# Two transformer blocks in sequence on one core: where an attention phase begins and ends among the projections around it

## The reference

```
mod = silu(c) @ ada_w + ada_b                    # shift, scale, gate
h = rmsnorm(x) * (1 + scale) + shift             # latent and context tokens
px, pc = split(h @ w_in)                         # q, k, v of A, B, C, and a gate
ya = softmax(rope(rmsnorm(q)) @ rope(rmsnorm(k)).T) @ v       # A: all keys
yb = softmax(q @ gathered_k.T + bias, q @ kc.T) @ v           # B: 2-D neighbourhood
yc = softmax(rope(q) @ banded_k.T, q @ kc.T, sink) @ v        # C: sliding window
x = x + gate * ((concat(ya, yb, yc) * silu(px[9])) @ w_out)   # context alike in layer 0
```

## Time and profile before

| | |
|---|---|
| profiled execution | 2545.05 us, of which the span of the trace 2543.2 |
| PE busy | 2439.3 us, 96% of the span |
| DVE, ACT, POOL busy | 1352.0, 950.8, 541.5 us |
| share of PE in the chain that ended last | 81% (DVE 8%, ACT 4%, issue 3%, POOL 2%) |
| projection of block 1 (L2380) on PE | 555.6 us |
| attention on PE (L575, L603) | 159.1 and 150.7 us |
| mean granted clock of TensorE | 0.992 of full speed |

### The profile page before, as it was taken

How to read it: one execution, slowest core, us unless ns; L and a number is a source line. 1 busy time by engine, 2 the same in 40 slices (tenths; PEclk the granted TensorE clock), 3 DMA queues, 4 the chain that set the end, 5 groups by cost and what they waited for, 6 DMA issues and landing times.

```text
span 2543.2 us, 38062 instructions
## 1 busy us (share of the span) xinstructions
PE 2439.3 (96%) x14758; PEld 1982.2 (78%) x14758; DVE 1352.0 (53%) x2731; ACT 950.8 (37%) x1751; POOL 541.5 (21%) x530
## 2 busy tenths in 40 slices
PE   6999999999998999999999999999999999999998
PEld 4777877878887778778778668888888767888887
DVE  3667756765407663666827745333335953533333
ACT  4464254452324542645335334222225333422222
POOL 2212222122243122221365232000003331100001
PEclk9999999999999999999999999999999999999999
DMA  7402422224124034132524112323323212223322
GB/s 270 145 2 75 174 63 72 84 94 178 57 79 166 26 125 158 39 133 95 190 85 145 51 57 68 106 77 114 98 81 103 71 53 72 83 84 107 100 83 75
DMA packets 66900, 250.36 MB, mean 98 GB/s; under 512 B 7969, under 2 KB 11553, under 8 KB 57377
## 3 DMA queue, kind: packets, MB, share of 16 engines
q1 hardware_dynamic: 62960, 236.36, 27.4%
q0 software_dynamic: 3248, 11.54, 1.4%
q10 hardware_dynamic: 512, 0.03, 0.0%
HBM read 243.67 MB, written 4.19 MB: 97 GB/s over the span
## 4 chain that ended last, share of the span: by engine, by line
PE 81%; DVE 8%; ACT 4%; issue 3%; POOL 2%; DVEq 1%; ACTq 0%; DMA 0%; SPq 0%; POOLq 0%
PE ps L2560 34%; PE ps L2380 20%; PE ps L575 5%; PE ps L603 5%; PE ps L643 4%; PE ps L2537 4%; DVE ps L1960 2%; ACT probs L797 2%; PE ps L2264 1%; PE ps L2361 1%; POOL split_panels_first L1059 1%; PE ps L2509 1%; PE ps L2399 1%; PE ps L2577 1%; PE ps L2309 0%
## 5 line engine op out<-in xcount | busy, mean ns | idle before, releaser
L2560 PE MATMUL ps<-h_split,split_panels 128*128 128x512 f32 x2928 | 685.7, 393 | 1.8 <-ACT projected L1506 0.8
L2560 PEld LDWEIGHTS ps<-h_split,split_panels 128*128 128x128 f32 x2928 | 545.9, 188 | 126.9 <-issue 13.7
L2380 PE MATMUL ps<-h_split_first,split_panels_first 128*128 128x512 f32 x2808 | 555.6, 355 | 9.0 <-DVE h_split_first L1828 4.9
L2380 PEld LDWEIGHTS ps<-h_split_first,split_panels_first 128*128 128x128 f32 x2808 | 453.5, 191 | 85.4 <-issue 7.8
L1059 POOL TENSOR_TENSOR split_panels_first<-panels_first,split_panels_first 128x1024 fp32r<-128x1024 f32 (+1 forms) x104 | 233.3, 2244 | 581.2 <-ACT split_panels_first L1249 581.2
L1905 DVE TENSOR_TENSOR split_panels<-panels,split_panels 128x1024 fp32r<-128x1024 f32 (+2 forms) x171 | 192.6, 1126 | 297.9 <-ACT split_panels L1257 294.2
L1257 ACT ACTIVATE split_panels<-panels 128x1024 fp32r<-128x1024 f32 (+2 forms) x210 | 204.3, 974 | 344.9 <-PE ps L2560 343.6
L1740 DVE SCALAR_TENSOR_TENSOR ps<-modulation_panels,silu_c,ps 128x256 f32<-128x256 f32 x480 | 225.1, 487 | 30.5 <-issue 2.1
L2560 PE MATMUL ps<-ffn_hidden_split,split_panels 128*128 128x512 f32 x990 | 225.0, 389 | 0.0
L2560 PEld LDWEIGHTS ps<-ffn_hidden_split,split_panels 128*128 128x128 f32 x990 | 185.8, 188 | 38.6
L1070 POOL TENSOR_TENSOR probs_turned<-probs_turned,probs 128x512 f32<-128x512 f32 x30 | 41.8, 1392 | 769.8 <-ACT probs L1449 769.8
(11 more groups left out here) (300 smaller groups left out, 2931.5 us busy)
## 6 DMA issues: line engine op xcount, KB each, us to landing
modulation_panels<-in_ada SPq DMA_DIRECT2D x64, 1024.0 KB, 5.0
panels<-in_w SPq DMA_DIRECT2D x88, 512.0 KB, 3.5
panels_first<-in_in SPq DMA_DIRECT2D x72, 512.0 KB, 5.8
panels<-in_in SPq DMA_DIRECT2D x42, 512.0 KB, 3.6
panels_first<-in_out SPq DMA_DIRECT2D x32, 384.0 KB, 3.0
panels<-in_w SPq DMA_DIRECT2D x32, 384.0 KB, 3.1
panels<-in_w SPq DMA_DIRECT2D x32, 320.0 KB, 2.8
panels<-in_out SPq DMA_DIRECT2D x16, 512.0 KB, 3.4
```

The source lines that it names most:

```text
L2380: ins = mm(at0, split1[:, s, w, c, :], hs1[:, h, c, lo:e], start=c == 0 and i == 0, stop=c == KC - 1 and i == 2)
L2560: ins = mm(out, split[:, n % SPLIT, a, c - base, :], moving(b, c), start=first and i == 0 and j == 0, stop=last and i == len(chunks) - 1 a ...
```

## The change

Four edits, all in the first block.

1. ACT: in the last block of a projection phase of A, B or C, the last `take_mod` and the two exponentials of unit 0 now stand ahead of the eviction of that block; behind it only the panel is rounded.
2. PE: the last modulation sum stands ahead of the scores of unit 0 and no longer behind the block's last chunk. `make_plan` numbers the turned tiles in the new order.
3. PE, order in the first steps: in A and C the turning of unit 0 stands ahead of the scores of unit 1 (`i == 1`); in all three mixers the outputs of unit 0 stand ahead of the turning of unit 1 (`i == 2`). In B the wait for the eviction moves from the scores of unit 1 to those of unit 2.
4. PE, exit: the latent products of two chunks of the next projection (three matmuls of 512 columns each, `latents_ahead`) go one ahead of the turning of the last unit, one between the last two outputs. The context products of these chunks stay where they were.

```diff
@@ make_plan
-        if before:
-            behind(before)
         if values_second and i == 1:
             step["values"] = values(groups[0][0], None)
+        (behind(before) now stands ahead of it)
@@ attention_pe
+                i = u["i"] if u else None
+                if m != "B" and i == 1:
+                    turn_probs_pe(pe, prev, o)
+                if i == 1:
+                    pe.wait_ge(mod_taken, ada_no[spare[l, last - 1]] + 1)
+                if i == (2 if m == "B" else 1):
+                    pe.wait_ge(proj_taken, NSEQ[l, last] + 1)
                 if u:
                     scores_pe(pe, u, o)
                 if u and step["values_first"]:
                     turn_values_pe(pe, step, o)
-                if prev:
+                if i == 2:
+                    turn_weights_pe(pe, old)
+                    outputs_pe(pe, old, o)
+                if u is None and old:
+                    latents_ahead(pe, l, NEXT[m], 0 if prev else 1)
+                if prev and not (m != "B" and i == 1):
                     turn_probs_pe(pe, prev, o)
...
-                if old:
+                if old and i != 2:
                     turn_weights_pe(pe, old)
                     outputs_pe(pe, old, o)
+        def latents_ahead(pe, l, m, c):
+            b = PHASES[m][0]
+            k, n = NSEQ[l, b], main_no[IN1, l, b]
+            if c == 0:
+                pe.wait_ge(rest1_done, n + 1)
+                pe.wait_ge(proj_taken, k - 1)
+            for i, (w, h) in enumerate(((0, 0), (0, 1), (1, 0))):
+                nc.tensor.matmul(bank(k % 2), split1[:, n % SPLIT1, w, c, :], hs1[:, h, c, 0:SEQ], start=c == 0 and i == 0, stop=False)
@@ attention_act
-                if u:
+                if u and (u["i"] > 0 or not u["in_sets"]):
                     exponentials_act(act, u, o)
@@ projected (ACT)
                         load_table(ACT.Exp)
+                        take_mod(spare[l, b - 1])
+                        first = next(step["unit"] for step in plans[l, m][0] if step["unit"])
+                        exponentials_act(act, first, Off(None))
                     act.wait_ge(proj_ready, k + 1)
@@ project (PE)
-                        block_chunk(l, b, n, c)
+                        block_chunk(l, b, n, c, m != "A" and j < 0 and c < AHEAD)
-                    if (l, b - 1) in spare:
+                    if (l, b - 1) in spare and not (m in "ABC" and b == PHASES[m][1] - 1):
                         sum_mod(spare[l, b - 1])
-                if m == "B":
-                    pe.wait_ge(proj_taken, k + 1)
-                    pe.wait_ge(mod_taken, ada_no[spare[l, b - 1]] + 1)
             def first_scores(l, m, k):
-                pe.wait_ge(*parts_made(ada_no[spare[l, PHASES[m][1] - 2]]))
+                sum_mod(spare[l, PHASES[m][1] - 2])
```

More of the change, by code:

```diff
@@ L166, in make_plan @@
         step = dict(unit=u, prev=before, old=two_back, values=[], values_first=values_second)
+        if before:
+            behind(before)
         if values_second and i == 1:
             step["values"] = values(groups[0][0], None)
-        if before:
-            behind(before)
         if values_second:
@@ L662, in attention_pe @@
                 u, prev, old = step["unit"], step["prev"], step["old"]
-                if m == "B" and u and u["i"] == 2:
+                i = u["i"] if u else None
[5 more added lines that the diff above has]
+                    pe.wait_ge(proj_taken, NSEQ[l, last] + 1)
+                if m == "B" and i == 2:
                     pe.wait_ge(values_taken, steps[0]["values"][1]["w"] + 1)
-                if m != "B" and u and u["i"] == 1:
-                    pe.wait_ge(proj_taken, NSEQ[l, last] + 1)
-                    pe.wait_ge(mod_taken, ada_no[spare[l, last - 1]] + 1)
                 if u:
@@ L831, in two_dit_blocks @@
         ADA1, ADA2, IN1, OUT1 = "ada1", "ada2", "in1", "out1"
+        NEXT = {"A": "B", "B": "C", "C": "G"}
+        AHEAD = 2
         second = [(ADA2, l, i) for l in range(DEPTH) for i in range(N_ADA2)]
@@ L1317, in projected @@
                             round_gated(l, c)
-                    if (l, b - 1) in spare and b != 1:
+                    if (l, b - 1) in spare and b != 1 and not (m in "ABC" and b == PHASES[m][1] - 1):
                         take_mod(spare[l, b - 1])
@@ L2371, in _, with block_chunk @@
             turn_mod(0)
-            def block_chunk(l, b, n, c):
+            def block_chunk(l, b, n, c, ahead=False):
                 k, s = NSEQ[l, b], main_no[IN1, l, b] % SPLIT1
@@ L2378, in block_chunk @@
                     for at0, lo, e in ((bank(k % 2), 0, SEQ), (bank(2 + k % 2, 0, CTX), SEQ, TOK)):
-                        if lo < n:
+                        if lo < n and not (ahead and lo == 0):
                             ins = mm(at0, split1[:, s, w, c, :], hs1[:, h, c, lo:e], start=c == 0 and i == 0, stop=c == KC - 1 and i == 2)
```

## The result

| | before | after |
|---|---|---|
| median of 9 runs each | 2549.18 us (2544.89 to 2556.15) | 2561.58 us (2556.82 to 2564.64) |
| ratio of the runs | | 1.0041, interval [1.0032, 1.0049] |
| profiled execution, span | 2545.05, 2543.2 us | 2561.93, 2560.1 us |
| mean granted clock | 0.992 | 0.987 |

The changed kernel is slower, by 0.3 to 0.5%. The forecast was 2558.8 us in a range of 2547 to 2569, with 0.76 for a difference within 0.5%. The time came out as forecast; one term of the sum, the clock, did not.

What follows compares the result with a forecast made beforehand. PE was taken as the bound, busy 2439.3 of 2543.2 us. Entries +10.7, exits -8.2 and clock +6.0 sum to +8.5 us, on the median of 2550.32 giving 2558.8, range 2547 to 2569.

Steps and rivals of the forecast that it cites:

- A, forecast +3.84 each: Entries of A0 and A1: PE waits for ACT's exponentials and DVE's copies, losing 3.84 us at each.
- B, +0.55 and -0.84: Entries of B0 and B1: PE waits 2.5 us for POOL's weights; +0.55 us at B0, -0.84 at B1.
- C, +1.86 and +1.43: Entries of C0 and C1: new PE waits for exponentials, weights and a DVE copy; +1.86 and +1.43 us.
- Exits, -8.2: Six phase exits: moved chunks of 0.73 us each fill PE's two gaps per exit; -8.2 us in all.
- A reading beside it: Context matmuls in a row at the exits: 11 to the microsecond, 0.09 us each, so they lose nothing.
- The clock, 4 falls x 1.5 = +6.0: Half-clock stretches behind the new long entry gaps: four at 1.5 us, +6.0 us, with 0 and 9 as ends.
- (b): Every new gap of 2.4 us and more brings a 1.7 us clock fall, six: +12.7, 2563.0 and up; chance 0.14.
- two of the four: Of the four gaps of 2.4 to 2.5 us (A0, A1, B0, B1), two bring a clock fall of 1.5 us.
- (a): The clock stays up behind the new gaps: 2545.05 + 2.5 us, or 2552.8 by the median; chance 0.22.
- (c): Exits give nothing, as PE then waits for DVE's modulation products in the next projection: 2567.0 us; chance 0.06.
- (d): Entries gain too, if DVE copies unit 0 before unit 1's row extremes: entries -13, exits -8, 2529 us; chance 0.04.

Runs made afterwards that it cites:

- copy-first variant: Changed kernel with DVE's copy of the turned group and weights of unit 0 ahead of unit 1's row extremes in A and C: 2546.68 us, ratio 0.9993 to before.
- exits-only trace: Kernel before plus only the two latent chunks of the next projection placed among the last unit's steps: 2538.73 us, ratio 0.9965 to before.
- entries-only kernel: Changed kernel without the chunks moved ahead at the exits: 2563.14 us, ratio 1.0063 to the kernel before.

## Why the prediction was right, and where it was off

- **A, forecast +3.84 each.** Shown. Gaps of 2.23, 3.24 and 0.87 us by the engines named; 3.81 without clock by the table; the copy-first variant takes the long gap away.
- **B, +0.55 and -0.84.** Shown: 0.68 and -0.72 where no fall comes. The second is so low in part because before had a fall at B1, worth 0.98 by the exits-only trace. The mechanism, POOL's queue, is shown by moving one instruction pair.
- **C, +1.86 and +1.43.** Measured 2.17 and 1.75, both 0.3 more. The hand schedule stopped at the scores of unit 3 and missed ACT's gap of 0.30 us behind them.
- **Exits, -8.2.** -7.9 in the changed kernel and -7.9 alone, nearly all of it. A reading beside it was wrong: the earlier trace rows counts the eleven products that touch that microsecond, some begun before it. Their starts lie 0.12 us apart, not 0.09. Among the others such a product takes the same 0.12 (0.35 a pair, less 0.23 for the one of 512 columns), so the conclusion, that they lose nothing, stands.
- **The clock, 4 falls x 1.5 = +6.0. This is the term that was mis-sized.** The profile has six, at 3.17 us a pair at A0 and 3.13 at A1 and 1.3 each at B: 20.4 less the 11.5 that the entries cost without (2 x 3.81, 0.68, -0.72, 2.17, 1.75), +8.9. The price of a fall was about right, the count was that of rival (b). What failed is "two of the four": in both profiles of this kernel it was four of four. Over all kernels with such gaps it was 13 of 20, so 2.6 of four, and 4.6 in all. Gaps of one execution aren't independent draws, so 13 of 20 is a rough figure. Why this kernel has more stays open.
- **What no term had.** G's long wait for DVE is 3.43 and not 2.95 us, so 0.48 of C1's exit is given back: DVE there doesn't get earlier with PE. With the exits alone it stayed 2.95, in the other variants it was 2.96 to 3.44; why wasn't tried. The projection of layer 1's A was 1.5 us longer (in the variants 0.3 to 1.7), with 17 us at half clock in place of 10. The second block, which the change doesn't touch, was 2.7 us longer, with half-clock stretches in other places than in the trace of before.
- **The sum.** By the trace 20.4 - 7.9 + 1.5 + 0.5 + 2.7 - 0.3 (ahead of A0) = +16.9 for a forecast of +8.5. Yet the medians differ by 12.4 and the ratio says 10.4: before's profiled execution lay 4 us below its median, after's on it. So 2558.8 was nearer to the median than its terms were to one trace, in part by luck.

Rival (a), a clock that stays up, is out; (b) was right in its count of falls. Its time, 2563.0, lies even nearer to the measured median of 2561.58 than the forecast's 2558.8; by the ratio, +10.4, its +12.7 is a little farther off than +8.5. So the time doesn't decide between the two, and the traces decide for (b). (c) and (d) are out. (d)'s condition, DVE's copy ahead of the row extremes, takes 12.9 us off the entries, but they still cost 7.5, where (d) had them at -13.

## What to carry to other kernels

When one engine's order is changed, the queues it waits on keep theirs: lay each of them anew for the first steps, and ask which instruction that was hidden now ends the wait. Here PE ran ahead on paper and waited for a DVE copy behind two copies that nobody needed yet, and for POOL's weights behind a panel. Moving the copy gave back 4.1 and 5.7 us at A and moving the weights 3.7 at each B, where the swap itself is worth 0.3. Price a new gap like these, of 2.2 us and more, with the half-clock stretch that may follow it: it did 23 times of 30. And split a change: its exits alone were worth 0.35%, its entries cost 0.6%.

## What the hardware showed that was not expected

The same gap, after the same instructions, brings a fall of the clock in one execution and none in another: 2.23 us at A0 in the changed kernel (clock 0.53 behind it) and 2.24 in the entries-only kernel (12 transposes in 1.53 us, full speed). Even the gap of 1.69 us of A, with none behind it in the kernel before, had one at both A entries of the exits-only kernel (+1.50 us each). Its stretch at A0:

```profile
129.00:131.00 2.00, 2.00 (x11) 1.91 (x10) 1.69 (x3) 0.59 (x1) 0.00 (x0) 0.50 0.00 0
```

The Trainium skill (TensorE: Matmul & The Clock Gate, "What's actually happening") has the clock judged in windows that run free of the kernel. These traces agree with it: whether a gap brings a fall differs between executions, and the two of the changed kernel, whose falls begin within 0.2 us of each other, have the same ones. And a wait that is to be filled with idle products is best filled from its start: with 2.55 us left open ahead of it the filler itself ran at half clock, twice of twice. With up to 0.4 us left open there was no fall in four places, but those had none unfilled either in the entries-only trace.
